# The final norm and the outputs' stores beside the last four experts of a mixture-of-experts encoder layer

## What is computed

```python
h = rms_norm(x, norm_ffn_g[layer])
x = x + expert_choice_ffn(h, w_router[layer], w_gate[layer], w_up[layer], w_down[layer])
...
return rms_norm(x, final_norm_g)

def expert_choice_ffn(h, w_router, w_gate, w_up, w_down):
    ...
    cap = max(1, EC_CAPACITY * n_tok // N_EXPERTS)
    ...
    g, idx = lax.top_k(aff.T, cap)
    xs = flat[idx]
    hid = jax.nn.silu(jnp.einsum('ecd,edf->ecf', xs, w_gate)) * jnp.einsum('ecd,edf->ecf', xs, w_up)
    out = jnp.einsum('ecf,efd->ecd', hid, w_down) * g[..., None].astype(h.dtype)
    y = jnp.zeros((n_tok, D), h.dtype).at[idx.reshape(-1)].add(out.reshape(-1, D))
```

## Time and profile before

| | |
|---|---|
| median of 3 runs | 2280.71 us (2280.4 to 2280.78) |
| the profiled execution, its own time | 2278.43 us |
| its span, first to last instruction | 2276.5 us |
| PE busy | 2024.2 us (89%) |
| DVE, ACT, POOL busy | 1461.5, 1108.2, 257.0 us |
| DMA traffic | 311.99 MB, mean 137 GB/s |

### The profile page before, as it was taken

The page is one execution under the profiler, slowest core; times in us unless marked ns, Lnnn a source line. Parts: engine busy times, 40 slices in busy tenths (PEclk is TensorE's granted clock), DMA queues, the critical chain, the costliest instruction groups (busy, mean ns, idle before and its releaser), DMA issues. The chain is left out here.

```text
span 2276.5 us, 44180 instructions
## 1 busy us (share of the span) xinstructions
PE 2024.2 (89%) x16048; PEld 1763.4 (77%) x16048; DVE 1461.5 (64%) x2748; ACT 1108.2 (49%) x1972; POOL 257.0 (11%) x398
## 2 busy tenths in 40 slices
PE   6999998899897899788899389999999999999990
PEld 5777776677776677566788289999999999999990
DVE  4376576666666467566338857777777777777763
ACT  4322222455555423266323156666666666666652
POOL 2001101000000011100122001111111111111101
PEclk9999999999998999799899689999999999999995
DMA  5211110100002111211233177777777777777756
GB/s 167 81 31 34 29 30 16 37 19 23 19 5 79 51 57 55 75 51 47 102 111 111 49 265 255 245 261 245 260 247 259 246 254 252 255 252 254 253 154 244
DMA packets 181872, 311.99 MB, mean 137 GB/s; under 512 B 11648, under 2 KB 81792, under 8 KB 181760
## 3 DMA queue, kind: packets, MB, share of 16 engines
q1 hardware_dynamic: 168832, 276.87, 36.3%
q0 software_dynamic: 7040, 25.17, 4.9%
q10 hardware_dynamic: 5888, 8.39, 1.0%
HBM read 276.83 MB, written 33.55 MB: 136 GB/s over the span
## 5 line engine op out<-in xcount | busy, mean ns | idle before, releaser
L2128 DVE TENSOR_TENSOR we_lo<-raw,we_hi 128x1024 fp32r<-128x1024 f32 x384 | 466.1, 1224 | 204.5 <-ACT we_hi L2074 203.6
L2040 PE MATMUL psum<-x_parts,we_hi 128*128 128x384 f32 x2048 | 586.3, 360 | 3.1 <-DVE we_lo L2128 3.1
L2042 PE MATMUL psum<-x_parts,we_lo 128*128 128x192 f32 x2048 | 513.9, 251 | 0.0
L2074 ACT CAST we_hi<-raw 128x1024 fp32r<-128x1024 f32 x384 | 400.3, 1054 | 174.5 <-PE psum L2042 101.7
L2042 PEld LDWEIGHTS psum<-x_parts,we_lo 128*128 128x128 f32 x2048 | 392.7, 192 | 0.6
L2040 PEld LDWEIGHTS psum<-x_parts,we_hi 128*128 128x128 f32 x2048 | 386.1, 189 | 4.1 <-issue 3.5
L587 PE MATMUL psum<-hT_hi,w_hi 128*128 128x512 f32 x512 | 215.7, 421 | 12.5 <-DVE w_lo L567 12.5
L589 PE MATMUL psum<-hT_hi,w_lo 128*128 128x512 f32 x512 | 203.1, 397 | 0.0
L588 PE MATMUL psum<-hT_lo,w_hi 128*128 128x512 f32 x512 | 202.9, 396 | 0.0
L587 PE MATMUL psum<-hP_hi,w_hi 128*128 128x512 f32 x256 | 111.0, 434 | 22.7 <-DVE w_lo L567 22.7
L587 PEld LDWEIGHTS psum<-hT_hi,w_hi 128*128 128x128 f32 x512 | 97.6, 191 | 34.3 <-DVE land L1100 7.5
(11 more groups left out here) (297 smaller groups left out, 3849.4 us busy)
## 6 DMA issues: line engine op xcount, KB each, us to landing
raw<-in_w_gate SPq DMA_DIRECT2D x128, 512.0 KB, 5.5
raw<-in_w_up SPq DMA_DIRECT2D x128, 512.0 KB, 6.0
raw<-in_w_down SPq DMA_DIRECT2D x128, 512.0 KB, 4.6
w_raw<-in_w_in SPq DMA_DIRECT2D x96, 256.0 KB, 2.8
y_rows<-x SPq DMA_DIRECT2D x12, 512.0 KB, 2.6
h_rows<-h SPq DMA_DIRECT2D x12, 512.0 KB, 2.9
y<-y_rows SPq DMA_DIRECT2D x12, 512.0 KB, 6.9
w_raw_s<-in_w_in SPq DMA_DIRECT2D x16, 256.0 KB, 3.0
```

Source lines behind the costliest of these rows:

```text
L2040: pe.matmul(out[:, 0:2 * SLOTS], w_hi[:, s, at], x_parts[p][:, k, :, :], start=(k == 0), stop=False, skip_group_check=True)
L2042: mm = pe.matmul(out[:, SLOTS:2 * SLOTS], w_lo[:, s, at], x_hi[p][:, k, :], start=False, stop=(k == DT - 1), skip_group_check=True)
L2074: act.copy(w_hi[:, n % PARTS, :], raw[:, s, :]).then_inc(hi.sem, 1)
L2128: dve.tensor_tensor(w_lo[:, n % PARTS, :], raw[:, n % RAW, :], w_hi[:, n % PARTS, :].bitcast(F32), ALU.subtract).then_inc(lo.sem, 1)
```

## The change

The block `finish` is gone. Its work stands in `experts`, in the steps of experts 12 to 15 (`LATE` = 4), which are written out; experts 0 to 11 stay in the loop.

- The 12 tiles of `y_rows` are loaded, squared, normed in place and stored while experts 12 to 14 and the start of 15 run. `of_tiles` gives the unit (counted from expert 12's first, 24 to an expert) in whose step a tile is squared; mean and norm follow one and two steps later. SP issues a tile's load two units behind it in its own order of weight loads, and its store ten units behind. A load waits for expert 11's rows (later tiles: for expert 12's and 13's) to be `written`.
- A tile that was loaded lacks what experts 12 to 15 add. So each late expert's 128 + 64 rows are gathered from `y_rows` once more behind its scatter (`fetch`), squared and normed (`of_late`), and scattered into the outputs over what stood there (`put`); the scatters wait for one another in the order of the experts, and the first for all tiles' stores.
- Expert 15's rows are fetched when expert 14's are written; its products are added to them on chip (`body("last")`), so that it has no scatter into `y_rows`.
- POOL makes the powers of all of these between its gathers and scatters (`late_steps`).
- The prompt rows' numbers without the offset of 1024 get a third plane of `index_cols`, by one more copy in the mixer.

```diff
                 dve.tensor_copy(gate_cols[:, 1 - t, :], SUMS[t][1][:, of]).then_inc(columns, 1)
+                if t:
+                    dve.tensor_copy(index_cols[:, 2, :], SUMS[t][0][:, of]).then_inc(columns, 1)
-def experts(nc, ctx, w_gate, w_up, w_down, ident, minus_half, psum, banks, index_cols, gate_cols, h2_dram, y_dram):
+def experts(nc, ctx, w_gate, w_up, w_down, g_final, ident, minus_half, psum, banks, index_cols, gate_cols, h2_dram, y_dram, out_p, out_s):
+    LATE, SLOTS_Y, NT = 4, 4, N_TOK // P
+    FIRST_LATE = EXPERTS - LATE
+    LOOPED = FIRST_LATE // 2
+    of_tiles = [16, 19, 22, 25, 28, 40, 43, 46, 49, 52, 71, 73]
+    of_late = [(66, 67), (75, 76), (90, 91)]
...
         index_both = sb("index_both", [P, 1], I32)
+        y, g_row, junk = sb("y", [P, SLOTS_Y, D]), sb("g_row", [P, D]), sb("junk", [P, D])
+        late_s, late_p = sb("late_s", [P, 2, D]), sb("late_p", [CAP_PROMPT, 2, D])
+        when = {**{q: u for q, u in enumerate(of_tiles)}, **{NT + 2 * f + part: us[part] for f, us in enumerate(of_late) for part in range(2)}}
+        in_turn = sorted(when, key=lambda q: when[q]) + [NT + 2 * LATE - 2, NT + 2 * LATE - 1]
+        rank = {q: n + 1 for n, q in enumerate(in_turn)}
+        beside = lambda u, later: [q for q in in_turn if when.get(q) == u - later]
+        def rows_at(q):
+            if q < NT:
+                return y[:, q % SLOTS_Y, :]
+            f, part = divmod(q - NT, 2)
+            return (late_p if part else late_s)[:, f % 2, :]
...
                         out.append(("turn", *next_of(i, p)))
-                out.append(("result", i, p))
+                    if late:
+                        u = (2 * i + p - FIRST_LATE) * UNITS + n
+                        out += [(kind, i, p, q) for later, kind in enumerate(("square", "mean", "norm")) for q in beside(u, later)]
+                out.append(("last" if last and p == 1 else "result", i, p))
...
-                def loads(i):
+                def load(t):
+                    s = t % SLOTS_Y
+                    if t == 0:
+                        sp.dma_start(g_row[:], g_final.partition_broadcast(P)).then_inc(g_in, 16)
+                    before = FIRST_LATE - 1 + max(0, of_tiles[t] - 5) // UNITS
+                    sp.wait_ge(written.sem, written.at(before // 2, before % 2))
+                    if t >= SLOTS_Y:
+                        sp.wait_ge(y_out[s], 16 * (t // SLOTS_Y))
+                    sp.dma_start(y[:, s, :], y_dram[t * P:(t + 1) * P, :]).then_inc(y_in[s], 16)
+                def store(t):
+                    s = t % SLOTS_Y
+                    to = out_s[t * P:(t + 1) * P, :] if t < T_SAMPLE // P else out_p[t * P - T_SAMPLE:(t + 1) * P - T_SAMPLE, :]
+                    sp.wait_ge(normed, rank[t])
+                    sp.dma_start(to, y[:, s, :]).then_inc(y_out[s], 16)
+                def loads(i, late):
...
                             sp.dma_start(to, src).then_inc(raw_in[s].sem, 16)
-                with sp.Fori(0, PAIRS) as i:
-                    loads(i)
+                            if late:
+                                u = (e - FIRST_LATE) * UNITS + n
+                                for t in range(NT):
+                                    if of_tiles[t] == u - 10:
+                                        store(t)
+                                for t in range(NT):
+                                    if of_tiles[t] == u - 2:
+                                        load(t)
+                with sp.Fori(0, LOOPED) as i:
+                    loads(i, False)
+                for i in range(LOOPED, PAIRS):
+                    loads(i, True)
+                for s in range(SLOTS_Y):
+                    sp.wait_ge(y_out[s], 16 * (NT // SLOTS_Y))
...
                                            scale=gate_cols[:, 1, bass.ds(2 * i + p, 1)]).then_inc(scaled_s.sem, 1)
+                    elif kind == "square":
+                        q = n
+                        if q < NT:
+                            act.wait_ge(y_in[q % SLOTS_Y], 16 * (q // SLOTS_Y + 1))
+                        elif q < NT + 2 * LATE - 2:
+                            f, part = divmod(q - NT, 2)
+                            act.wait_ge(late_in[f % 2][part], 16 * (f // 2 + 1))
+                        else:
+                            act.wait_ge(last_sum, (2, 6)[(q - NT) % 2])
+                        if rank[q] > 1:
+                            act.wait_ge(squared, rank[q] - 1)
+                        rows = rows_at(q)
+                        act.activation(junk[0:rows.shape[0], :], rows, ACT.Square, accum_out=column(ss, q)).then_inc(squared, 1)
+                    elif kind == "last":
+                        act.wait_ge(used.sem, used.at(i, p * UNITS + UNITS - 1))
+                        act.wait_ge(scaled_p.sem, scaled_p.at(i, 2 * p - 1))
+                        for h in range(2):
+                            act.activation(low_rows[:, h * BLK:(h + 1) * BLK], half(p, "down")[h][CAP_PROMPT:P, :], ACT.Copy,
+                                           scale=gate_cols[CAP_PROMPT:P, 0, EXPERTS - 1:EXPERTS]).then_inc(scaled_low.sem, 1)
+                        for q in in_turn[-2:]:
+                            body("square", i, p, q)
...
                                                      low_rows[:, h * BLK:(h + 1) * BLK], ALU.mult, ALU.add).then_inc(scaled_p.sem, 1)
+                    elif kind == "mean":
+                        dve.wait_ge(squared, rank[n])
+                        dve.tensor_scalar(column(ms, n), column(ss, n), 1.0 / D, EPS, ALU.mult, ALU.add).then_inc(mean, 1)
+                    elif kind == "norm":
+                        rows = rows_at(n)
+                        if rank[n] == 1:
+                            dve.wait_ge(g_in, 16)
+                        dve.wait_ge(powed, rank[n])
+                        dve.scalar_tensor_tensor(rows, rows, column(rstd, n), g_row[0:rows.shape[0], :],
+                                                 ALU.mult, ALU.mult).then_inc(normed, 1)
+                    elif kind == "last":
+                        of_s, of_p = in_turn[-2:]
+                        f, e = LATE - 1, slice(EXPERTS - 1, EXPERTS)
+                        dve.wait_ge(used.sem, used.at(i, p * UNITS + UNITS - 1))
+                        dve.wait_ge(late_in[f % 2][0], 16 * (f // 2 + 1))
+                        for h in range(2):
+                            part = rows_at(of_s)[:, h * BLK:(h + 1) * BLK]
+                            dve.scalar_tensor_tensor(part, half(p, "down")[2 + h][:], gate_cols[:, 1, e], part,
+                                                     ALU.mult, ALU.add).then_inc(last_sum, 1)
+                        dve.wait_ge(late_in[f % 2][1], 16 * (f // 2 + 1))
+                        for h in range(2):
+                            part = rows_at(of_p)[:, h * BLK:(h + 1) * BLK]
+                            dve.scalar_tensor_tensor(part, half(p, "down")[h][0:CAP_PROMPT, :], gate_cols[0:CAP_PROMPT, 0, e], part,
+                                                     ALU.mult, ALU.add).then_inc(last_sum, 1)
+                        body("mean", i, p, of_s)
+                        for h in range(2):
+                            part = rows_at(of_p)[:, h * BLK:(h + 1) * BLK]
+                            dve.wait_ge(scaled_low.sem, scaled_low.at(i, 2 * p + h))
+                            dve.wait_ge(last_sum, 3 + h)
+                            dve.tensor_tensor(part, part, low_rows[:, h * BLK:(h + 1) * BLK], ALU.add).then_inc(last_sum, 1)
+                        body("norm", i, p, of_s)
+                        body("mean", i, p, of_p)
+                        body("norm", i, p, of_p)
...
-                def with_gathers(i, last):
+                def power(q):
+                    pool.wait_ge(mean, rank[q])
+                    pool.tensor_tensor(column(rstd, q), column(ms, q), minus_half[0:column(ms, q).shape[0], 0:1], ALU.pow).then_inc(powed, 1)
+                def fetch(f):
+                    e = FIRST_LATE + f - (f == LATE - 1)
+                    pool.wait_ge(written.sem, written.at(e // 2, e % 2))
+                    column_of = slice(FIRST_LATE + f, FIRST_LATE + f + 1)
+                    for part, (rows, of) in enumerate(((late_s, index_cols[:, 1, column_of]), (late_p, index_cols[0:CAP_PROMPT, 0, column_of]))):
+                        if f >= 2:
+                            pool.wait_ge(late_out[f % 2][part], 16 * (f // 2))
+                        pool.indirect_dma_start(rows[:, f % 2, :], None, y_dram, bass.IndirectOffsetOnAxis(ap=of, axis=0)
+                                                ).then_inc(late_in[f % 2][part], 16)
+                def put(f):
+                    column_of = slice(FIRST_LATE + f, FIRST_LATE + f + 1)
+                    if f == 0:
+                        for s in range(SLOTS_Y):
+                            pool.wait_ge(y_out[s], 16 * (NT // SLOTS_Y))
```

(29 more changed lines are left out.)

85 lines of the change are left out of this document (23 added, 62 removed).

## The result

The changed kernel took **2242.5 us** in the median of 4 runs (2241.5 to 2244.6), the kernel before, timed beside it, 2280.6: a ratio of 0.983, 95% interval 0.9816 to 0.9843. The gain is 38.1 us where 43.5 were forecast; 2242.5 lies within the range of 2233 to 2250 and 5.3 us above the forecast. The profiled execution took 2244.6 us with a span of 2242.8, where 2233.0 was forecast: 9.8 us to explain.

The account below looks back on a forecast made before the run. PE bounds the experts; 57.9 us behind its last matmul overlap nothing. With the norm beside PE at zero cost, a new tail from 2218.6 ends the span at 2233.0 instead of 2276.5, gaining 43.5: median 2237.2 us, range 2233 to 2250.

Parts of the forecast that it names:

- What the change removes: Behind PE's last matmul: the whole 57.9 us tail goes, with expert 15's scatter, the block's end and the tiles' traffic.
- Eighteen pieces beside PE at zero: Experts 12 to 15: norm work on twelve tiles and three experts' rows fits in the engines' free time, costing PE nothing.
- The port rule: POOL's powers and DVE's two-input instructions exclude each other: up to 0.96 us per power, 17 us of DVE waits, none on PE.
- POOL's scatters 16 us into the next expert: Scatters of experts 12 to 14 start about 16 us into the next expert instead of 3, behind the group's powers.
- The turned rows with 2 to 11 us of room: Next expert's gathered rows land 32 to 41 us in, likeliest 38; PE wants them at 43.1, so cost zero.
- The last fetch at 2212.8: Last expert: the final gather of rows waits only for the last power behind the last split, and is issued at 2212.8.
- rival 2: GpSimd's chain of puts and fetches in the last expert runs late, PE loses up to 1 us: 2241 to 2247, 20%.
- The landings, 7.2 and 4.8 us: New tail: the last sample and prompt scatters land 7.2 and 4.8 us after issue, at 2232.8 and 2232.3.
- With 0.2 us from the last landing to the end: Program's end: 0.2 us from the last scatter's landing to the span's end at 2233.0.
- DMA as the bound, 3%: Late experts: DMA becomes the bound, gain gone below 275 GB/s, kernel slower below 270: 2286 us and up; 3%.
- the forecast's own rival: First of the listed rivals, the forecast itself: PE never waits; 2233 to 2241 us, likeliest 2237.2; 62%.

Follow-up runs that it names:

- all three edits: Changed kernel plus scatters of experts 12 to 14 issued early, fetch 3 ahead of two powers, GpSimd drain behind fetches 0 and 1: 2232.7 us, 0.9781 of the kernel before.

## Why the prediction came out as it did

**What the change removes: right.** The whole tail of the earlier trace rows is gone from behind PE.

**Eighteen pieces beside PE at zero: right, but for the turned rows below.** PE's stretch grew by 1.4 us in one execution and 0.3 in the other, and by nothing in five of the edited kernels (221.5 to 221.7); no split waited for `raw`.

**The port rule: agrees, at no cost.** Of the 20 powers of the changed kernel 13 start beside a DVE instruction with two SBUF inputs and take 1.45 to 2.66 us, mostly 1.46; the six that run while DVE idles take 0.55 to 0.58, as in the final norm of before. That put DVE 4.2 us behind in nine waits, against the bound of 17, and nobody on PE's path. The Trainium skill, "SBUF — State Buffer", section "SBUF: two separate sides", also warns that a DMA issued by GpSimd can't write its descriptors while DVE runs an instruction of a two-port performance mode. That sentence does not name instructions with two SBUF inputs, such as the norms and splits of this kernel; issues beside these are longer here all the same. The issue of put 3's sample rows took 2.02 us with DVE's norm of the prompt rows running, 1.99 for put 1's at 2209.01 beside a split of 1.22 us from 2208.91 on, and 1.00 for put 2's at 2221.37, where DVE idles until 2223.82. This is read from rows; no run here took DVE away from an issue.

**POOL's scatters 16 us into the next expert: right for two of three.** Counted from each expert's own start (the `low_rows` of the one before), those of experts 12, 13 and 14 started at 16.7, 16.8 and 18.9 us; the power in front of the third took 2.66 us where 0.55 was put.

**The turned rows with 2 to 11 us of room: wrong, by the gather's landing above all.** The wait is behind expert 12's scatter, which started when it was forecast. The scatter then took 13.8 us (2069.27 to 2083.06; at most 13.2 forecast), and the sample rows' gather was issued 33.7 us into expert 13 (28 to 33 forecast) and landed 10.6 us later, where 7.3 was taken and 8.5 was the bound: 44.3 us in. Why it landed so late is not shown. The norm's traffic raised the engines' share in this expert from 0.77 to 0.98, but in the kernel before this gather landed 6.1 us after issue with the share at 1.03 around it (2070 to 2079). In the six runs with the scatters at the old place and no extra loads this gather landed 42.6 to 44.3 us in, and PE waited by just what it came after 42.9: 1.4, 0.2, 1.1, 1.0 and twice nothing. In the three with early scatters it landed 37.3 to 39.0 us in and PE never waited, so that edit is a cure.

**The last fetch at 2212.8: mis-sized by 5.0, of which 3.1 against PE's own end, and that cost 2.9.** This is rival 2 (20%) in its place, but not in its damage: PE's splits were not held, only the last fetch was. The forecast costed this fetch from the last split alone and took the queue ahead of it as done. Putting it ahead of the two powers restores the forecast's start.

**The landings, 7.2 and 4.8 us: mis-sized by -1.8 on the chain's end.** They were read from scatters that add. Plain ones land 4.4 and 3.5 us after issue; the run with scatters that add puts the difference on the addition.

**"With 0.2 us from the last landing to the end": wrong, by 6.8 us, the largest error.** Nothing in the rows gives it. Behind the last landing of the kernel before lies the end of the final norm's block, which has no indirect DMA; there the DMA engines move nothing from 2274.8 on and the last store's landing is signalled at 2275.1, so that even this end was 1.4 us and not 0.2. The right row stood in the trace: from the scatter's landing at 2231.1 to the next block's first load at 2236.99 lie 5.9 us, which the prediction counted as removed with the tail. 4.6 of them are the drain that closes a block with 56 of GpSimd's DMAs unsettled, and the new kernel has 70, 5.8 us, in the block that now ends the program. No rival had this. The kernel with all three edits has a tail of 14.3 where the prediction wrote 14 to 15, but that is luck: 2.4 us instead of 0.2 at the end make up for landings 1.8 earlier.

**DMA as the bound, 3%: right.** The four experts ran at 0.80 to 1.03 of the engines without a late weight, expert 14 at 351 GB/s. The room left was not measured; a sixth more traffic, in the order of that run, cost 22.9 us.

**The number: in the range, in part by luck.** The mechanism of the forecast holds: the tail went beside PE and PE's work did not grow. But 2242.5 lies outside the 2233 to 2241 of the forecast's own rival, in the stretch that rival 2 was given for another damage. The largest error is the 6.8 us of a term that no rival had. Had the landings not been 1.8 us quicker than put, and the two profiled executions not 4.4 us apart from their medians, the same errors would make 2248.8, near the end of the range.

## What to carry over

Read the time behind the last landing at the end of the block that will end the program, not at the end that the program has now: what GpSimd must still settle goes with its DMAs, and a drain of GpSimd in a stretch where it idles takes it off the end. Put it where nothing waits for GpSimd: ahead of the fetches it held them back, and PE paid for it in a wait and in clock. On an in-order queue the last transfer is as late as the sum of all steps ahead of it, so cost it from the queue's order and move what needs nothing from its neighbours to the front. An operation that the trace lacks (a scatter that only writes) deserves one bound from the like operation without its extra work, or the sum inherits it.
